# Products of constants on TensorE inside the norms of a four-layer block

## What is computed

```python
def first_block(x, c, ...):
    cond = silu(c)
    for l in range(2):
        sh1, sc1, gt1, sh2, sc2, gt2 = split(cond @ w_mod[l] + b_mod[l], 6)
        h = rms_norm(x, norm_g[l, 0]) * (1.0 + sc1) + sh1
        y = mixer_block(h, ...)                    # h @ w_in, four mixers, @ w_o
        x = x + gt1 * rms_norm(y, norm_g[l, 1])
        h = rms_norm(x, norm_g[l, 2]) * (1.0 + sc2) + sh2
        y = square(relu(h @ w_up[l])) @ w_down[l]
        x = x + gt2 * rms_norm(y, norm_g[l, 3])
    return x

def second_block(x, c, ...):                       # layers 2 and 3: y is not normed
    for l in range(2):
        h = rms_norm(x, norm_mix[l]) * (1 + sc_m) + sh_m
        y = hybrid_mixer(h, ...) if l % 2 == 0 else retention_mixer(h, ...)
        x = x + gt_m * y
        h = rms_norm(x, norm_ffn[l]) * (1 + sc_f) + sh_f
        x = x + gt_f * swiglu(h, ffn_w_in[l], ffn_w_out[l])
    return x
```

## Time and profile before

| | |
|---|---|
| median of 3 runs | 1775.62 us (1774.39 to 1776.91) |
| profiled execution, whole time | 1780.66 us |
| its span, first to last instruction | 1778.9 us |
| mean granted clock of TensorE | 0.917 of full speed |
| PE busy | 1544.0 us (87%) |
| DVE busy | 1069.0 us (60%) |
| ACT busy | 744.5 us (42%) |
| POOL busy | 336.1 us (19%) |

### The profile page before, as it was taken

How to read it: one execution, slowest core, us unless ns; L and a number is a source line. 1 busy time by engine, 2 the same in 40 slices (tenths; PEclk the granted TensorE clock), 3 DMA queues, 4 the chain that set the end, 5 groups by cost and what they waited for, 6 DMA issues and landing times. The chain is left out here.

```text
span 1778.9 us, 26844 instructions
## 1 busy us (share of the span) xinstructions
PE 1544.0 (87%) x11710; PEld 1479.1 (83%) x11710; DVE 1069.0 (60%) x1253; ACT 744.5 (42%) x805; POOL 336.1 (19%) x243
## 2 busy tenths in 40 slices
PE   2897679998898679999795886899888998889989
PEld 2896579998787579999795775899888997889988
DVE  6765767787455458687575524667694443455534
ACT  3533355434543355533664312544225443354432
POOL 0000210143000101043000202022444600302232
PEclk8998789999898689999898876999899999999999
DMA  9560548787240229788241002477693541436550
GB/s 396 219 258 1 223 190 331 300 338 261 87 154 21 95 91 357 292 340 316 95 166 71 1 1 73 188 286 292 255 363 129 181 176 70 166 133 227 210 181 33
DMA packets 47206, 336.68 MB, mean 189 GB/s; under 512 B 5360, under 2 KB 5744, under 8 KB 6768
## 3 DMA queue, kind: packets, MB, share of 16 engines
q1 hardware_dynamic: 46224, 333.09, 50.0%
q10 hardware_dynamic: 864, 1.87, 0.3%
HBM read 333.89 MB, written 1.05 MB: 188 GB/s over the span
## 5 line engine op out<-in xcount | busy, mean ns | idle before, releaser
L416 DVE TENSOR_TENSOR weights_hi_lo<-ring,weights_hi_lo 128x2048 fp32r<-128x2048 f32 x213 | 510.1, 2397 | 425.6 <-ACT weights_hi_lo L410 424.7
L410 ACT ACTIVATE weights_hi_lo<-ring 128x2048 fp32r<-128x2048 f32 x213 | 407.3, 1913 | 638.0 <-PE PS L510 329.9
L510 PE MATMUL PS<-hi,weights_hi_lo 128*128 128x256 f32 x3200 | 589.6, 287 | 41.5 <-DVE lo L609 28.0
L510 PEld LDWEIGHTS PS<-hi,weights_hi_lo 128*128 128x128 f32 x3200 | 507.6, 195 | 46.1 <-issue 30.6
L749 PE MATMUL PS<-acts_hi_lo,weights_hi_lo 128*128 128x256 f32 x3552 | 449.4, 290 | 47.3 <-POOL acts_hi_lo L702 26.4
L749 PEld LDWEIGHTS PS<-acts_hi_lo,weights_hi_lo 128*128 128x128 f32 x3552 | 443.1, 198 | 55.1 <-issue 29.9
L510 PE MATMUL PS<-lo,weights_hi_lo 128*128 128x256 f32 x1600 | 457.5, 286 | 0.0
L510 PEld LDWEIGHTS PS<-lo,weights_hi_lo 128*128 128x128 f32 x1600 | 311.4, 195 | 0.0
L427 DVE CUSTOM_DVE_ANT_0 ring<-ring,cond 128x1024 f32<-128x1024 f32 x192 | 257.0, 1377 | 0.9 <-DMA smallS<-in_small_dram 0.9
L510 PE MATMUL PS<-weights_hi_lo,hi 128*128 128x256 f32 x1248 | 228.7, 285 | 12.0 <-DVE weights_hi_lo L416 8.0
L700 POOL CAST acts_hi_lo<-arena 128x512 fp32r<-128x512 f32 x74 | 73.8, 997 | 716.8 <-PE PS L749 354.0
(11 more groups left out here) (331 smaller groups left out, 1184.7 us busy)
## 6 DMA issues: line engine op xcount, KB each, us to landing
ring<-in_stream_dram SPq DMA_DIRECT2D x313, 1024.0 KB, 4.9
constS<-in_const_dram SPq DMA_DIRECT2D x1, 1856.0 KB, 11.3
cond<-in_rows_dram SPq DMA_DIRECT2D x2, 512.0 KB, 5.6
arena<-in_x_dram ACTq DMA_DIRECT2D x1, 1024.0 KB, 12.4
smallS<-in_small_dram SPq DMA_DIRECT2D x1, 883.0 KB, 12.6
out_dram<-arena ACTq DMA_DIRECT2D x2, 256.0 KB, 2.4
out_dram<-arena SPq DMA_DIRECT2D x2, 256.0 KB, 2.9
constS<-in_const_dram SPq DMA_DIRECT2D x1, 320.0 KB, 13.3
```

The costliest lines, as they stand in the source:

```text
L410: act.activation(wsp[:, g % 2, 0, :], ring[:, n % RING, :], ACT.Copy).then_inc(*hi_ready.one())
L416: dve.tensor_tensor(wsp[:, g % 2, 1, :], ring[:, n % RING, :], wsp[:, g % 2, 0, :].bitcast(F32), ALU.subtract).then_inc(used["dve"], 1)
L510: mm = pe.matmul(o, lhs, rhs, start=k + g + j == 0, stop=k == KD - 1 and j == 2, skip_group_check=True)
```

## The change

A helper `idle_products` issues f32 products of the identity matrix and 256 columns of the table of constants into bank 2 of PSUM, each with its own start and stop, so that nothing accumulates and nothing reads it. In every norm seven of them stand behind the last sum. In the norms of layers 0 and 1 one more stands behind the sums of each of the first three pairs. That makes 4 x 10 + 4 x 7 = 68 products. They wait for nothing and signal nothing.

```diff
@@ -575,11 +575,19 @@
+            def idle_products(pe, n):
+
+                for _ in range(n):
+                    pe.matmul(PS[:, 2, 0:SEQ], ident, constS[:, 0:SEQ], start=True, stop=True)
+
             def pe_part(pe):
                 for b in range(4):
                     pe.wait_ge(*xsq.at(b + 1))
                     pe.matmul(PS[:, 1, 0:SEQ], ones, sq[:, b % 2, 0:SEQ], start=b == 0, stop=False)
                     pe.matmul(PS[:, 1, 0:SEQ], ones, sq[:, b % 2, SEQ:512], start=False, stop=b == 3).then_inc(*xsum.one())
+                    if b < 3 and l < 2:
+                        idle_products(pe, 1)
+                idle_products(pe, 7)
```

## The result

| | before | changed |
|---|---|---|
| median, first chip | 1775.01 us (4 runs, 1770.03 to 1776.91) | 1797.46 us (4 runs, 1794.05 to 1797.75) |
| median, another chip | 1780.22 us (23 runs, 1770.05 to 1789.93) | 1796.36 us (6 runs, 1795.56 to 1803.68) |
| ratio on record, 95% interval | | 1.0105 [1.0077, 1.0132]; the other chip 1.0093 [1.006, 1.0126] |
| profiled execution, its span | 1780.66, 1778.9 us | 1794.05, 1792.3 us |

The changed kernel is about 1% slower, 17 to 19 us by the ratios. The medians on the first chip lie 22.5 us apart, still inside that ratio's interval. It was forecast slower, but by 11 us, and the measured 1797.46 us lies above the range's end of 1793.

The account below looks back on a forecast made before the run. PE was taken as the bound from the second slot on, whose start an ACT and DVE chain behind the sums decides. 0 + 6.0 + 5.1 = 11.1 us on the median 1775.62 gave 1786.7 us, range 1779.5 to 1793.

Parts of the forecast that it names:

- the slow first slot was hidden: Behind each norm: PE's half-clock first slot still ends 0.78 us before the second slot can start (second norm).
- The gain is nothing: Behind the norms: seven products make the first slot end sooner, but the second starts as before; 0 us.
- the hole before the second slot grows: PE's idle time between first and second slot grows from 0.78 to about 2.8 us.
- One sign of being right: Norms of layers 0 and 1: the logarithm's (L593's) wait for PE grows by about 1.3 us each.
- the falls of the clock: Second slots: half clock after the longer idle time in four of seven norms, 1.5 us each, 6.0 us.
- The rule weighed in the prediction: Idle gaps of PE up to about 3 us are harmless, so the clock term before second slots would be 0.
- the sums: Norms of layers 0 and 1: three single products delay the last sum by 1.28 us, four times, 5.1 us.
- the sum of 11.1 us: Whole kernel: 0 for the first slots, 6.0 for clock falls before second slots, 5.1 for later sums.
- The clock did not hold: Rival, second slots: clock stays full through 2.8 us of idleness, only the sums cost; 1780.7 us, chance 0.18.
- the first slot was not on the path: Rival, behind norms: an earlier first slot end pulls everything forward, up to 16 us less 5.1; 1764.7 us, chance 0.05.
- the delays did not vanish in the projections: Rival: delays of layers 0 and 1 vanish in the projections, no measurable change; 1775.6 to 1779 us, chance 0.08.
- "Dearer": Rival, norms: the seven run at half clock or falls last longer, 19.5 us; 1795 us, chance 0.07.

Follow-up runs that it names:

- e4: Changed kernel without the single products, with five (ten in layer 1's projections) more products behind the first slot of projection and up phases; 1.0013 of before.
- e7: Kernel before with fifteen products of constants behind each norm's last sum, no single products between the sums; 0.9989 of before.
- e5: The changed kernel measured again on another chip, nothing altered; 1796.36 us, 1.0093 of before.
- e1: Changed kernel without the single products, only the seven behind each norm's last sum kept; 1788.9 us, 1.0065 of before.
- e3: Changed kernel plus five products (ten in layer 1's projections) behind the first slot of every projection and up phase; 1791.81 us, 1.0059 of before.
- e2: Changed kernel without the seven products, only the single ones between the sums of layers 0 and 1 kept; 1788.92 us, 1.0056 of before.
- e9: Kernel before with the products of e6 and e7, and ten more ahead of the sums of x in layers 0 and 1; 0.9966 of before.
- e6: Kernel before with none in norms, 48 products ahead of exposed stretches (output, down, layer 1's projections); 1772.63 us, 0.9958 of before.

## Why the prediction was right or wrong

**Right: the slow first slot was hidden, and the second slot's start is fixed.** In every trace it comes 12.9 to 13.1 us after the last sum (15.3 to 15.4 us in the third norm), with the first slot slow, fast or late. "The gain is nothing" held: e4 and e7 are within their intervals of before.

**Right: the hole before the second slot grows.** Forecast 2.8 us, measured 2.58 to 2.61 us in seven norms, and 4.95 us in the third.

**One sign of being right failed.** The logarithm's wait for PE was to grow by about 1.3 us in each norm of layers 0 and 1. It grew from 2.2 us in four norms to 4.4 us in five (in e5, to 3.3 us in four). ACT's fourth square now waits for PE itself and stands 0.85 us later against the first sum, so the table load behind it is late as well. That square before and in the changed kernel:

```profile
239.26 0.63 ACT L590 ACTIVATE arena<-X 128x512 f32<-128x512 f32 x1 [0.90 <-DVE X L819]
240.04 0.63 ACT L598 ACTIVATE arena<-X 128x512 f32<-128x512 f32 x1 [1.75 <-PE PS L587]
```

What shows the delay is the stretch from the first to the last sum, which grew by 1.27 us here.

**Right in kind, under-sized: the falls of the clock.** Each cost 1.5 us as worked out. I took four in seven, 6.0 us. Three traces gave five, six and four, 15 of 21, so 7.5 us. The third norm I put at nothing, because it has its fall already. Its hole grew from 3.16 to 4.95 us, and it also ran longer at half clock (4.35 us shown here and more behind it):

```profile
466.95:471.30 4.35, 4.34 (x20) 4.35 (x21) 2.15 (x1) 0.10 (x1) 0.00 (x0) 0.50 0.75 267
```

That is 5.2 us in all against 3.4 before, about 0.8 us more (3.8 us at half clock in e1, 5.8 in e5). The rule weighed in the prediction, of the Trainium skill's "TensorE: Matmul & The Clock Gate", section "Why this matters for your kernels", by which holes under about 3 us do no harm, is not borne out by this case: holes of 2.6 us let the clock fall 15 times in 21.

**Right in kind, under-sized: the sums.** 5.1 us forecast, 5.65 us in the traces, 5.8 us between the traces of e3 and e4. The timing of e2 gives 10 us with an interval from 5.7 to 14 us.

**Wrong: the sum, by three of its terms, and the range around it.** The step that failed first is the sum of 11.1 us: the falls were put at 6.0 us and gave 7.5, the third norm was put at nothing and gave 0.8, and the sums were put at 5.1 us and gave 5.65. Together that is 14.0 us, of the measured 17.6 (the mean of the two ratios less one, 0.99% of 1775 us). On the median of 1775.62 us it would be 1789.6, still inside the range, so these terms alone did not carry the time out of it.

The second step that failed is the one that put the sum on the median and gave width to the terms only and none to the base. The three runs of before lay within 2.5 us. Over 26 runs on one other chip single executions of the same kernel lie between 1770.49 and 1789.0 us, and the four runs of before on the first chip already span 7 us. The remaining 3.6 us of the 17.6 (8.5 us, if the medians of the first chip are taken) lie within the intervals of the ratios (13.7 to 23.4 us on the first chip, 10.7 to 22.4 on the other). Whether they are a cost or the spread stays open. e4, at 1.0013, shows no cost of the seven products themselves (its interval ends at 0.33%, 6 us). The single products could hold it, since their timings stand above their traces, but no run tells. The profiles differ by 13.4 us, close to 14.0, and that is partly luck: in this pair the sums of the first four norms differ by 4.1 us, and a faster pace gave back 1.3 us (below).

**Wrong rivals.** The clock did not hold, the first slot was not on the path, and the delays did not vanish in the projections. "Dearer", 1795 us, came nearest to the measured number, but not by its own cause. The seven products ran at full clock in every norm, the first slot was not pushed back, and the clock fell in five second slots and not in all seven.

## What to carry to other kernels

A stretch at half clock is worth mending only where it is exposed: look for the wait that ends behind it. If PE idles again before its next piece of work for another engine's sake, a faster stretch only moves the idle time, and the clock may then fall in a place that counts. Work for nothing may be put into a hole if it fills it nearly to its end, does not stand ahead of something another engine waits for, and has behind it a dense stretch in which PE is the bound.

## What the hardware showed that was not expected

**No sharp length of a hole decides.** Some other holes between dense products stand in the same places of all eleven traces. Behind one of 1.40 to 1.48 us, which every trace has twice, the clock never fell, in 22 places. Behind one of 2.45 to 2.60 us in the output product of layer 0 it fell in all eleven. Behind one of 2.15 us in the down product of layer 2 it held in nine traces, as in the kernel before, and fell in e7 and e9. In e7, first in order of time, then by windows:

```profile
1284.52 0.74 PE L755 MATMUL PS<-acts_hi_lo,weights_hi_lo 128*128 128x256 f32 x4 [2.15 <-DVE weights_hi_lo L416]
1284.50:1287.90 3.40, 3.38 (x20) 3.38 (x21) 3.40 (x3) 0.00 (x0) 2.58 (x2) 0.69 1.01 371
```

And behind the hole of 2.79 us that follows in the same phase the clock fell in ten of eleven, and held in e7. So the 2.15 us that did no harm in the trace of before could have done some, and a count over many traces is a better ground for such a term than five places of one.

**The same mixer takes 40 or 45 us.** The mixer of layer 0, with sparse work on PE, by windows in the kernel before and in e2, whose code there is the same:

```profile
142.89:159.70 16.81, 14.37 (x109) 12.59 (x109) 7.29 (x26) 2.44 (x7) 0.00 (x0) 0.85 0.00 1
159.71:183.11 23.40, 17.68 (x113) 16.01 (x113) 13.50 (x26) 9.68 (x37) 0.00 (x0) 0.76 0.00 1
```

```profile
143.22:158.80 15.58, 13.97 (x109) 12.44 (x109) 7.23 (x26) 2.44 (x7) 0.00 (x0) 0.83 0.00 1
158.88:187.92 29.04, 22.67 (x112) 20.26 (x113) 13.54 (x26) 9.63 (x37) 0.00 (x0) 0.62 0.00 1
```

The second stretch is 23.4 us with a clock of 0.76 in the mean, or 29.0 us with 0.62. Before, the changed kernel, e1, e6, e7 and e9 had the short one, the other five the long one. It isn't the program that decides: e5 is the changed kernel again and has the long one.

```profile
161.02:190.05 29.03, 22.66 (x113) 20.27 (x113) 13.49 (x26) 9.63 (x37) 0.00 (x0) 0.62 0.00 1
```

So 5.6 us can come or go between two executions in this place alone. That it makes a good part of the spread of 19 us is likely but not shown, as nearly all executions that were timed have no profile.

**The pace at full clock differs by 1%.** DVE's halves of neighbouring slots, which PE's pace sets in the up phase of layer 2, in the kernel before:

```profile
1142.89 2.29 DVE L416 TENSOR_TENSOR weights_hi_lo<-ring,weights_hi_lo 128x2048 fp32r<-128x2048 f32 x1 [3.57 <-ACT weights_hi_lo L410]
...
1148.58 2.29 DVE L416 TENSOR_TENSOR weights_hi_lo<-ring,weights_hi_lo 128x2048 fp32r<-128x2048 f32 x1
```

and in the changed kernel:

```profile
1154.15 2.29 DVE L416 TENSOR_TENSOR weights_hi_lo<-ring,weights_hi_lo 128x2048 fp32r<-128x2048 f32 x1 [4.94 <-ACT weights_hi_lo L410]
...
1159.79 2.29 DVE L416 TENSOR_TENSOR weights_hi_lo<-ring,weights_hi_lo 128x2048 fp32r<-128x2048 f32 x1
```

5.69 us a slot against 5.64, both at a granted clock of 1.00, and so through the whole phase. Over its 22 slots this gave the changed kernel's profile back 1.3 us, about what the fall in its second slot had cost. e5, the same program, has 5.70 us a slot there. Why the pace differs was not tried.
